# Key norms inside block four, pair 0's inverse earlier, and attention scores between turned weights and outputs

## The reference

```
xn   = rms_norm(x)
proj = xn @ w_in                       # 6 parts of 1024: dq dk dv | rr rk rv
o_da = diff_attention(dq, dk, dv)      # 8 heads, 2 score maps each, causal, ALiBi; a = p0 - lam*p1; o = a @ v; per-head norm
o_rw = rwkv7_time_mix(xn, rr, rk, rv)  # 16 heads of 64; r, k, v mixed with the token before;
                                       # kk = k*k_k / max(norm(k*k_k), 1e-12); delta-rule state, group norm, gate
h    = x + concat(o_da, o_rw) @ w_out
h    = h + hier_moe(rms_norm(h))       # 32 experts of 2048 -> 512 -> 2048 (gate, up, down), top 2 in the best group
out  = rms_norm(h) * g_final
```

## Time and profile before

| | |
|---|---|
| median of 3 runs | 1616.26 us |
| the profiled execution's own time | 1614.82 us |
| its span, first to last instruction | 1612.9 us |
| busy share of PE, DVE, ACT, POOL | 84%, 29%, 20%, 3% |
| moved by DMA | 481.05 MB, mean 298 GB/s over the span |
| chain that ended last | PE 53%, DMA 40%, DVE 4%, ACT 1% |
| mean granted TensorE clock | 0.915 of 2.4 GHz |

### The profile page before, as it was taken

How to read it: one execution, slowest core, us unless ns; L and a number is a source line. 1 busy time by engine, 2 the same in 40 slices (tenths; PEclk the granted TensorE clock), 3 DMA queues, 4 the chain that set the end, 5 groups by cost and what they waited for, 6 DMA issues and landing times.

```text
span 1612.9 us, 22483 instructions
## 1 busy us (share of the span) xinstructions
PE 1359.0 (84%) x9370; PEld 723.2 (45%) x9370; DVE 465.4 (29%) x1086; ACT 320.3 (20%) x742; POOL 42.8 (3%) x91
## 2 busy tenths in 40 slices
PE   7999999999999989987877867877776876877865
PEld 6888878888887444532322322222222221222221
DVE  6032356676653651321101201201101101111103
ACT  1012122333322331121211211211111111111112
POOL 2000010000010000000000000000000000000000
PEclk9999999999999999997977977978878888988887
DMA  9433322222224329489999999999999999999995
GB/s 306 152 105 104 105 79 79 80 80 80 80 81 169 100 87 415 175 360 428 432 430 435 432 431 432 432 435 431 431 431 432 435 431 432 430 432 434 430 431 230
DMA packets 61911, 481.05 MB, mean 298 GB/s; under 512 B 8550, under 2 KB 27639, under 8 KB 48919
## 3 DMA queue, kind: packets, MB, share of 16 engines
q1 hardware_dynamic: 60962, 478.89, 72.9%
q10 hardware_dynamic: 884, 1.23, 0.2%
HBM read 478.01 MB, written 2.10 MB: 298 GB/s over the span
## 4 chain that ended last, share of the span: by engine, by line
PE 53%; DMA 40%; DVE 4%; ACT 1%; issue 1%; DVEq 0%; SPq 0%; POOL 0%; ACTq 0%
DMA ring<-in_moe_w_gate_dram 22%; DMA ring<-in_moe_w_up_dram 16%; PE ps L929 11%; PE ps L741 9%; PE ps L1158 8%; PE ps L1008 6%; PE ps L1177 3%; PE ps L1134 3%; PE ps L820 2%; DMA ring<-in_moe_w_down_dram 2%; PE ps L1185 2%; PE ps L958 1%; PE ps L1169 1%; PE ps L808 1%; PE ps L884 1%
## 5 line engine op out<-in xcount | busy, mean ns | idle before, releaser
L1158 PE MATMUL ps<-ring,oT 128*32 128x512 f32 x2048 | 340.1, 826 | 205.3 <-DMA ring<-in_moe_w_gate_dram 115.4
L1158 PEld LDWEIGHTS ps<-ring,oT 128*32 128x32 f32 x2048 | 83.6, 144 | 458.4 <-issue 312.5
L929 PE MATMUL ps<-xT,ring 128*128 128x256 f32 x768 | 190.7, 391 | 0.0
L2035 DVE TENSOR_TENSOR oT<-oT,ps 128x128 f32<-128x128 f32 x32 | 9.2, 288 | 590.3 <-ACT oT L1524 590.3
L929 PEld LDWEIGHTS ps<-xT,ring 128*128 128x128 f32 x768 | 138.6, 189 | 23.5 <-issue 3.6
L741 PE MATMUL ps<-xT,ring 128*128 128x256 f32 x640 | 139.4, 380 | 0.0
L741 PEld LDWEIGHTS ps<-xT,ring 128*128 128x128 f32 x640 | 121.2, 190 | 17.8 <-issue 1.5
L1177 PE MATMUL ps<-ring,oT 128*32 128x512 f32 x1024 | 118.4, 603 | 8.5 <-DVE oT L2035 8.2
L1008 PE MATMUL ps<-ring,oT 128*128 128x512 f32 x256 | 114.2, 597 | 1.9 <-DVE oT L1816 1.1
L1134 PE MATMUL ps<-xT,oT 128*32 128x512 f32 x512 | 115.3, 1030 | 0.4 <-DVE oT L2023 0.4
L1169 PEld LDWEIGHTS ps<-fold,oT 128*128 128x128 f32 x512 | 59.6, 192 | 39.7 <-issue 39.7
(11 more groups left out here) (327 smaller groups left out, 1228.0 us busy)
## 6 DMA issues: line engine op xcount, KB each, us to landing
ring<-in_moe_w_gate_dram SPq DMA_DIRECT2D x32, 4096.0 KB, 32.5
ring<-in_moe_w_up_dram SPq DMA_DIRECT2D x32, 4096.0 KB, 33.0
ring<-in_moe_w_down_dram SPq DMA_DIRECT2D x31, 4096.0 KB, 32.6
ring<-in_w_in_dram SPq DMA_DIRECT2D x24, 1024.0 KB, 5.2
ring<-in_w_in_dram SPq DMA_DIRECT2D x32, 768.0 KB, 4.6
ring<-in_w_out_dram SPq DMA_DIRECT2D x16, 1024.0 KB, 5.2
ring<-in_moe_w_down_dram SPq DMA_DIRECT2D x2, 2048.0 KB, 30.8
res<-in_x_dram SPq DMA_DIRECT2D x2, 1024.0 KB, 6.9
```

Of the source, the lines that this page charges most:

```text
L929: last = mm(ps[:, 6 + (par + c) % 2, 0:S], wv[:, k, c * P:(c + 1) * P], xT[:, kq * KQ + k, :], start=(kq == 0 and k == 0), stop=(kq == 3 a ...
L1158: last = mm(ps[c * B:(c + 1) * B, 1 + j, :], xe[:, par, k, :], w[:, k, :], start=(kq == 0), stop=(kq == 3), tile_position=(0, c * B))
```

## The change

Key sums: the eight products move from behind block 4 to behind its first quarter. On ACT the roots, `exps(0)`, `exps(1)` and the state scales now come before the copies of block 4; `exps(1)` waits for `r_prep`. On DVE the norms of keys 1 and 2, `decay_sums(1)` and `plain_factors(1, 1)` come before `mix_block(4)`. POOL's staging of v waits on a new semaphore `s_vmix` that DVE raises after `mix_block(4)`.

Pair 0's preparation in block 5's loop: `products` ahead of step 2 (was 4), `bonus` ahead of 4 (6), the inverse ahead of 6 to 13 (7 to 14), `turn_vb` ahead of 14 (15), `turn_k` ahead of 15 (after the loop). ACT's `token_k` comes before its last copy of block 5.

Attention: `scores` is split in `turn_values` and `scores`, `attend` in `turn_weights` and `attend`. The scores of head h + 2 stand between the turned weights and the outputs of head h. DVE does `head_weights(h)` before `head_max(h + 1)` and adds the finished tile before `head_output`. ACT does `head_exps(h + 1)` right after copying the turned weights of head h.

Experts: load 4 is split in two halves. The first half waits only for the first two of four quarters of the first gate product (`m_part`), and PE waits for it on `m_fifth`. SP's first 12 loads of the loop are written out.

```diff
         s_nst = sem("kk_norms_rooted")
+        s_vmix = sem("first_v_blocks_mixed")
...
         m_ring = [sem(f"expert_slot_landed_{s}") for s in range(MSLOTS)]
+        m_part = sem("half_of_first_gate_read")
+        m_fifth = sem("first_half_of_fifth_weights_landed")
         m_last = sem("first_half_of_last_weights_landed")
...
             first_chunks(MSLOTS - LEAD, MSLOTS)
-            with sp.Fori(0, 7) as i:
+            s = (MSLOTS + LEAD) % MSLOTS
+            sp.wait_ge(m_part, 1)
+            sp.dma_start(mslot(s, 1, MSLOT)[:, 0, 0:MSLOT // 2], wu_t[:, 1, 0:MSLOT // 2]).then_inc(m_fifth, 16)
+            sp.wait_ge(m_read, 1)
+            sp.dma_start(mslot(s, 1, MSLOT)[:, 0, MSLOT // 2:], wu_t[:, 1, MSLOT // 2:]).then_inc(m_ring[s], 16)
+            for n in range(MSLOTS + 1, MSLOTS + 4 * CHUNKS):
+                sp.wait_ge(m_read, n - MSLOTS + 1)
+                s = (n + LEAD) % MSLOTS
+                load_chunk(s, slice(n // CHUNKS, n // CHUNKS + 1), n % CHUNKS, m_ring[s])
+            with sp.Fori(1, 7) as i:
                 for q in range(MSLOTS, MSLOTS + 4 * CHUNKS):
...
             copy_factors(0, 0)
-            pool.wait_ge(r_g, 2)
+            pool.wait_ge(s_vmix, 1)
             g.tensor_copy(vst, projR[:, 2 * MT, :]).then_inc(r_vst, 1)
...
+            def key_sums():
+                pe.wait_ge(s_l3, 3 * MT)
+                for m in range(MT):
+                    if m % 2 == 0:
+                        pe.wait_ge(s_sq, m // 2 + 1)
+                    last = mm(ps[:, 4 + m // 2, (m % 2) * S:(m % 2 + 1) * S], same64[:, :], tmp[:, m, :], start=True, stop=True)
+                    if m % 2:
+                        last.then_inc(s_nrm, 1)
...
                     last.then_inc(s_free, 1)
+                    if outs and kq == 0:
+                        key_sums()
                     if fold and kq == 0:
...
             rkv_block(4, outs=True)
-
-            pe.wait_ge(s_l3, 3 * MT)
-            for m in range(MT):
-                if m % 2 == 0:
-                    pe.wait_ge(s_sq, m // 2 + 1)
-                last = mm(ps[:, 4 + m // 2, (m % 2) * S:(m % 2 + 1) * S], same64[:, :], tmp[:, m, :], start=True, stop=True)
-                if m % 2:
-                    last.then_inc(s_nrm, 1)
             heads = [slice(0, L), slice(L, P)]
...
                 c, kq = i // 4, i % 4
-                if i == 4:
+                if i == 2:
                     pe.wait_ge(s_prA, 4 * RB)
                     products(0, 0)
-                elif i == 6:
+                elif i == 4:
                     bonus(0, 0)
-                elif 7 <= i < 15:
-                    inverse(0, i - 7)
+                elif 6 <= i < 14:
+                    inverse(0, i - 6)
+                elif i == 14:
+                    turn_vb(0, 0)
                 elif i == 15:
-                    turn_vb(0, 0)
+                    turn_k(0, 0)
                 if c == 0:
...
                     last.then_inc(s_pr, 1)
-            turn_k(0, 0)
             pe.wait_ge(s_prA, 4 * RB + 3)
...
-            def scores(h):
+            def turn_values(h):
                 if h > 1:
...
                 last.then_inc(t_vt, 1)
+            def scores(h):
                 if h > 1:
...
-            def attend(h):
+            def turn_weights(h):
                 pe.wait_ge(t_a, h * 2 + 2)
...
                 last.then_inc(t_at, 1)
+            def attend(h):
                 vtok = vtoks[h % 2]
...
             scores(0)
+            turn_values(0)
             rwkv_halves(1)
...
             scores(1)
+            pe.wait_ge(t_vta, 1)
+            turn_values(1)
             for h in range(MT):
                 rwkv_halves(HALVES[h])
+                turn_weights(h)
+                if h + 2 < MT:
+                    scores(h + 2)
                 attend(h)
                 if h + 2 < MT:
-                    scores(h + 2)
+                    turn_values(h + 2)
             rwkv_halves(2 * MT)
...
-            def gate_up(s, par, j):
+            def gate_up(s, par, j, kqs=range(4)):
                 w = mslot(s, KT, DE)
-                for kq in range(4):
+                for kq in kqs:
                     for c in range(G4):
...
+                if u == 1:
+                    pe.wait_ge(m_fifth, 16)
                 gate_up(landed(1), par, 1).then_inc(m_read, 1)
...
             pe.wait_ge(m_cnt, 1)
-            gate_up(LEAD, 0, 0).then_inc(m_read, 1)
+            gate_up(LEAD, 0, 0, (0, 1)).then_inc(m_part, 1)
+            gate_up(LEAD, 0, 0, (2, 3)).then_inc(m_read, 1)
             with pe.Fori(0, NB - 1) as i:
...
                     a.copy(gate[:, 4 * half + i, :], ps[:, 4 * (1 - half) + i, 0:S]).then_inc(s_l3, 1)
-            rkv_copies(4)
             for b in range(4):
...
             state_scales(0)
+            act.wait_ge(r_prep, 1)
+            exps(1)
+            state_scales(1)
+            rkv_copies(4)
             last_block_copy(0)
-            exps(1)
-            act.wait_ge(r_g, 2)
-            state_scales(1)
             power(0, 0)
+            power(0, 1)
             last_block_copy(1)
-            power(0, 1)
             power(0, 2)
...
             token_vb(0, 0)
+            token_k(0, 0)
             last_block_copy(3)
-            token_k(0, 0)
...
             head_v(1)
-            head_exps(1)
             for h in range(MT):
...
                 a.copy(aT.rearrange("p a b -> p (a b)"), ps[:, 6, 0:3 * P]).then_inc(t_ata, 1)
+                if h + 1 < MT:
+                    head_exps(h + 1)
                 if h + 2 < MT:
...
                     a.activation(osq, otok[:, h + t * MT, :], ACT.Square, accum_out=ssq[:, h + t * MT:h + t * MT + 1]).then_inc(t_osq, 1)
-                if h + 2 < MT:
-                    head_exps(h + 2)
             act.wait_ge(t_osq, 2 * MT + 1)
...
             decayed_factors(0, 0, first=True)
+            key_norms(1)
+            unit_keys(1)
+            decay_sums(1)
+            plain_factors(1, 1)
+            key_norms(2)
+            unit_keys(2)
             mix_block(4)
+            own.join()
+            dve.sem_inc(s_vmix, 1)
             mask_products(0, 0)
             triangles(0, 0)
-            decay_sums(1)
             bonus(0, 0)
             power(0, 0)
-            key_norms(1)
             power(0, 1)
-            unit_keys(1)
-            plain_factors(1, 1)
             power(0, 2)
...
             whole_inverse(0, 0)
-            key_norms(2)
-            unit_keys(2)
...
             group_output(MT - 1)
+            head_weights(0)
             head_max(1)
-            head_weights(0)
             for h in range(1, MT + 1):
+                add_tiles(HALVES[h - 1] // 2)
                 head_output(h - 1)
-                add_tiles(HALVES[h - 1] // 2)
+                if h < MT:
+                    head_weights(h)
                 if h + 1 < MT:
                     head_max(h + 1)
-                if h < MT:
-                    head_weights(h)
             dve.wait_ge(s_sst, 1)
...
```

## The result

The changed kernel takes 1599.97 us (median of 4 runs, 1599.42 to 1600.35) against 1616.30 (4 runs); the ratio is 0.9901 with a 95% interval of [0.9888, 0.9914]. That is 16.3 us faster. The profiled execution took 1600.15 us, its span 1598.2.

What follows compares the result with a forecast made beforehand. PE bounds the front, the expert load stream from load 4 the rest. Terms 4.1 + 6.1 + 1.8 = 12.0 us take 1616.26 to a forecast of 1604.3 us, range 1602.6 to 1607.6.

Steps and rivals of the forecast that it cites:

- Block four and pair 0: Block 5 of the projection: earlier key sums, norms and pair 0 steps remove PE's waits, 4.1 us.
- the four waits: PE in block 5: bonus 0.3, first inverse step 1.9, fourth step 1.0, first solve 0.9 us; all forecast to go.
- Rival A: Pair 0's inverse: round trips catch 0.3 us in six places, last wait kept; 1607.0 us; 12 in 100.
- Attention: Attention stretch: three terms of removed or shortened PE waits, 6.1 us in sum, lower bound 3.9.
- The three mechanisms: Attention: scores cover the weights' copy (3.9), weights come before PE (1.9), group output chain starts earlier (0.3 us).
- (a): Attention, heads 0 to 5: scores fill PE's waits for ACT's copy of the turned weights; 3.9 us.
- (b): Attention, ahead of heads 2, 4, 6: DVE's new order removes PE's waits for the weights; 1.9 us.
- Rival B: Attention: weights become late through a closed DVE, PE, ACT, DVE chain, so their waits stay; 1606.2 us; 10 in 100.
- Load 4 in halves: Expert stage start: first half issued 1.77 us sooner, second queues without a gap; gain 1.8 us, bounds 0 and 1.8.
- Rival C: Load 4: halves gain nothing, 1606.1 us; 6 in 100, of which 2 for a lost 0.2 us, 1606.3.
- Rival D: Expert stream: 1.34% slower loses all 12.0 us, over 1.7% makes the kernel over 0.2% slower; 2 in 100.
- E: Output projection: first loads set PE's pace and absorb gains in front, only load 4's part left; 1614.5 us; 3 in 100.

Runs made afterwards that it cites:

- before_c: The kernel before with no edit, profiled for one more trace; the text gives no total time for it.

## Why the prediction was wrong, point by point

**Block four and pair 0.** Right in its mechanism: the four waits went, no new one is printed, the first solve came at 225.2 (forecast 226.6; 1.1 of the difference is the earlier start of that execution). Forecast 4.1, measured 4.4 between the first two traces. Rival A, round trips that bite in the inverse, showed only in small: the third and fourth steps start 0.1 and 0.2 us later behind their quarter step than the others (203.86 and 207.00 in the timeline), and the third did so before.

**Attention.** The three mechanisms were right: the remaining waits are the ones that the prediction named, and head 7's weights were ready 0.4 us ahead of PE, as worked out. The term that was mis-sized is the worth of a wait: I took (a) and (b) at their printed 3.9 + 1.9 = 5.8, and they gave 7.9. Nine waits, each 0.23 us dearer than printed. My upper bound, "6.1 above, plus 0.3", took the printed idle time as a ceiling. It is not one. Rival B did not occur.

**Load 4 in halves.** Forecast 1.8, measured 3.88 - 1.98 = 1.90, and stage G stayed at 887.7 to 888.1, so the stream moved as a whole. Rival C fell. The Trainium skill, "DMA: Bandwidth & Descriptors", section "Anatomy of one DMA", gives a fixed 2 us for a DMA issued by GpSimd; the prediction wrote "every DMA", while these loads are issued by SP. This trace shows no such loss between two DMAs of one queue, since the stream after two halves is as long as after one load.

**The sum.** The step that failed is the pricing of the waits: the prediction counted a removed wait at its printed idle time and took that for the most it could give. It put (a) and (b) of the attention at 5.8 and the waits of block 5 at 4.1; they gave 7.9 and 4.4. With 0.1 each at load 4 and in the pair stages, the stages gave 14.6 us where the sum had 12.0. These stages alone put the time at 1616.3 - 14.6 = 1601.7, already below my range. Each gain in front did pass through the expert stream to the end.

The other 1.7 us had no term at all. I put everything outside my terms at nothing, working from one execution of 1614.82 us, which happened to have the short end and the undisturbed clock, and added the 1.4 us between it and the median to both kernels alike. By the traces that was the part that can differ: the drop of the clock in block 5, 1.65 us in two of seven traces that have the wait of 1.9 us, is in no trace without it, and the end after the stream was 1.5 us longer on the mean in the kernel before. Whether that end is shorter because of the change, or by chance in three traces, stays open: the clock of the last products is shown, its cause is not. Rival D, a slower stream, and E, absorbed gains, did not occur.

Two small sums were off without an effect: 92 loads of 4 MB (4.19 million bytes) at 432 GB/s take 893 us and not 897, and the 850 us stretch holds some 87 loads, so that PE idles 2.4 us per load and not 2.3.

**Router stage.** Not in my sum: E took 82.38 instead of 81.91 in one of the three traces of the changed kernel, and in two of five of the kernel before, so it is scatter that both kernels have.

## What to carry to other kernels

A wait of TensorE cost more than its printed idle time here, because the product ahead no longer overlaps its end with the next one: 0.23 us for each wait of the attention, whatever released it, which for waits of 0.6 us is a third, and some 0.1 for each in block 5. How much to add can be read from the trace: the duration of the product ahead, less the distance from its start to the next start where nothing waits (0.16 and 0.07 us here). So an upper bound from printed idle time is too low. Before forecasting from a single execution, ask which of its stages had the granted clock below 1.00 in other executions. Here the wait of 1.9 us was such a place, and no trace without the wait had the drop.

## What the runs showed of the hardware

Stages A and D repeat within 0.1 us between the traces of one kernel where the granted clock is 1.00 in them. The timed runs of the kernel before scatter from 1614.7 to 1619.3 us, and its five traces show where executions differ: the first products (block 0 begins at 14.9 to 16.1), the router stage (81.9 us, or 82.4 with the granted clock at 0.94 from 660 to 687 us in before_c), block 5 with the granted clock down to 0.74 behind idle time in two (1.65 us), and the last products (stage H, 13.4 to 16.3 us, with a granted clock of 0.58 in the slow case). The stream of 91 loads of 4 MB from load 4's issue to the last up product took 887.6 to 888.2 us in all traces.
